# Search's end, the last maxima and eight modulation columns placed elsewhere on VectorE; TensorE multiplies constants in front of long waits

## What is computed

```python
for l in range(2):
    sh1, sc1, ga1, sh2, sc2, ga2 = split(silu(c) @ w_ada[l] + b_ada[l], 6)   # modulation, 48 columns of 128
    z = (rmsnorm(x, g1) * (1 + sc1) + sh1) @ w_in[l]
    a_out = u * (w_spatial @ standardize(v))        # chunked gating
    score = sum_h(wi[h] * relu(qi[h] @ ki.T))       # index scores, top 256 keys of each query are kept
    b_out = softmax(q @ k.T over the kept keys) @ v # prompt in blocks of 128, sampled rows over 2048 cached keys + 32
    c_out = silu(standardize(conv31(a * sigmoid(g))) * g_cn)
    x = x + ga1 * (concat(a_out, b_out, c_out) @ w_out[l])
    x = x + ga2 * ((silu(h2 @ w_gate) * (h2 @ w_up)) @ w_down)    # h2 = rmsnorm(x, g2) * (1 + sc2) + sh2
y = rmsnorm(x, g_final)
```

## Time and profile before

| | |
|---|---|
| median of 3 runs | 3053.58 us (3050.45 to 3053.7) |
| the profiled execution's own time | 3048.94 us |
| its span, first to last instruction | 3047.2 us |
| mean granted TensorE clock | 0.971 |
| PE busy | 2833.2 us (93%) |
| VectorE (DVE) busy | 1649.6 us (54%) |
| ScalarE (ACT) busy | 986.9 us (32%) |
| GpSimd (POOL) busy | 643.2 us (21%) |
| DMA queue of SP | 219.36 MB, 21.4% of 16 engines |

### The profile page before, as it was taken

How to read it: one execution, slowest core, us unless ns; L and a number is a source line. 1 busy time by engine, 2 the same in 40 slices (tenths; PEclk the granted TensorE clock), 3 DMA queues, 4 the chain that set the end, 5 groups by cost and what they waited for, 6 DMA issues and landing times.

```text
span 3047.2 us, 42621 instructions
## 1 busy us (share of the span) xinstructions
PE 2833.2 (93%) x15994; PEld 2448.6 (80%) x15994; DVE 1649.6 (54%) x2788; ACT 986.9 (32%) x1260; POOL 643.2 (21%) x278
## 2 busy tenths in 40 slices
PE   4998879889999999999979988898999999999996
PEld 2778733369999999999977875333999999999996
DVE  7768777683452444534544777763444335353355
ACT  4246646422221111111233564562332111111112
POOL 1411500001122222121242033000112222212221
PEclk9999989989999999999989999998999999999998
DMA  5412100251221222212241311002112222222222
GB/s 215 136 64 84 36 21 0 63 182 48 83 79 59 83 76 76 100 59 83 70 139 45 122 43 36 0 1 63 35 56 85 79 75 78 74 84 71 81 82 85
DMA packets 71352, 224.93 MB, mean 74 GB/s; under 512 B 17233, under 2 KB 17489, under 8 KB 70097
## 3 DMA queue, kind: packets, MB, share of 16 engines
q1 hardware_dynamic: 70192, 219.36, 21.4%
q10 hardware_dynamic: 1056, 4.19, 0.3%
HBM read 211.44 MB, written 11.54 MB: 73 GB/s over the span
## 4 chain that ended last, share of the span: by engine, by line
issue 45%; PE 35%; DVE 7%; ACT 6%; POOL 4%; DVEq 2%; DMA 1%; ACTq 0%; POOLq 0%; SPq 0%
PE ps L952 33%; ACT notsel L751 4%; POOL w_lo L591 4%; PE ps L998 1%; DVE hf L1344 1%; DMA w_ada<-in_w_ada 1%; PE ps L1059 1%; DVE ada_later L1363 1%; DVE ada_junk L1363 0%; DVE junk L1363 0%; DVE w_ada L1363 0%; DVE s_keep L1482 0%; DVEq L1472 0%; DVE s_cand L1470 0%; DVEq L1373 0%
## 5 line engine op out<-in xcount | busy, mean ns | idle before, releaser
L591 POOL TENSOR_TENSOR w_lo<-w_raw,w_hi 128x1024 fp32r<-128x1024 f32 x202 | 498.3, 2467 | 2282.3 <-ACT w_hi L702 2282.3
L952 PE MATMUL ps<-u_hi,w_hi 128*128 128x352 f32 (+1 forms) x2112 | 457.4, 325 | 2.1 <-ACT rstd L903 2.1
L952 PE MATMUL ps<-u_hi,w_lo 128*128 128x352 f32 (+1 forms) x2112 | 458.4, 325 | 0.0
L952 PE MATMUL ps<-u_lo,w_hi 128*128 128x352 f32 (+1 forms) x2112 | 455.6, 324 | 0.0
L702 ACT CAST w_hi<-w_raw 128x1024 fp32r<-128x1024 f32 x202 | 211.0, 1045 | 534.1 <-PE ps L952 314.6
L952 PEld LDWEIGHTS ps<-u_hi,w_hi 128*128 128x128 f32 x2112 | 362.1, 189 | 3.7 <-ACT rstd L903 2.7
L952 PEld LDWEIGHTS ps<-u_hi,w_lo 128*128 128x128 f32 x2112 | 361.0, 189 | 0.0
L952 PEld LDWEIGHTS ps<-u_lo,w_hi 128*128 128x128 f32 x2112 | 361.0, 189 | 0.0
L751 ACT ACTIVATE notsel<-score,s_cand 128x384 bf16<-128x384 f32 (+3 forms) x248 | 297.5, 1200 | 134.4 <-DVE s_cand L1470 134.3
L1778 DVE SCALAR_TENSOR_TENSOR x<-ps,mod,x 128x704 f32 (+2 forms) x240 | 125.4, 578 | 362.0 <-PE ps L952 355.6
L1363 DVE SCALAR_TENSOR_TENSOR junk<-w_ada,cond_row 128x1024 f32<-128x1024 f32 x104 | 219.9, 2114 | 26.8 <-issue 24.1
(11 more groups left out here) (261 smaller groups left out, 4120.3 us busy)
## 6 DMA issues: line engine op xcount, KB each, us to landing
w_ada<-in_w_ada SPq DMA_DIRECT2D x96, 512.0 KB, 4.9
w_raw<-in_w_up SPq DMA_DIRECT2D x88, 512.0 KB, 3.5
w_raw<-in_w_in SPq DMA_DIRECT2D x34, 512.0 KB, 3.6
ada_later<-in_w_ada SPq DMA_DIRECT2D x32, 512.0 KB, 3.5
cw<-in_convw SPq DMA_DIRECT2D x32, 512.0 KB, 5.2
w_raw<-in_w_down SPq DMA_DIRECT2D x32, 384.0 KB, 3.1
w_raw<-in_w_down SPq DMA_DIRECT2D x32, 320.0 KB, 2.9
w_raw<-in_w_out SPq DMA_DIRECT2D x16, 512.0 KB, 3.5
```

What stands on the lines that cost most here:

```text
L591: nc.gpsimd.tensor_tensor(w_lo[slot][:], w_raw[:], w_hi[slot][:].bitcast(F32), ALU.subtract)\
L952: last = nc.tensor.matmul(ps[:, bank + t, 0:w], wt[slot][:, kk, :], mv[:, kk, t * TW:t * TW + w], start=(at == 0 and p == 0), stop=(at == ...
```

## The change

- A helper `keep_warm(n, bank)` issues n products of 128x128 by 128x512 of bf16 constants into a bank of PSUM whose contents are not used. TensorE issues them: 16 in front of strip 0 of layer 0 (behind a new wait for the modulation), 26 in front of and 26 behind the sum of squares at the start of layer 1, 26 in front of the last one, and in each layer 14 in front of the waits of the index strip, 14 in front of the first mean (behind a new wait for the convolution's last group but one), and 5 in front of the third sampled chunk and 5 in front of the first transposed sampled chunk.
- `finish_search(0, PSRCH)` moves from between the two `gate_rows` to behind `diagonals(0)`. TensorE's wait for v_ready moves behind the first logits.
- In the sampled selection `diagonals(7)` moves to behind the scan, ahead of the selection's last three instructions. The filling of vcache with ones moves from VectorE to GpSimd.
- Layer 0's last eight modulation columns (the gate of the feed-forward part) leave the sampled stage: ten columns stand in front of the output of block 7 instead of thirteen, and six behind the first m_lo instead of eleven. The eight are made in the output projection, one behind each strip's u_lo, from a buffer of their own, and SP loads one behind each of the next weight strips (the first behind a wait for the last sampled product, the others behind a wait for the column before). Their bias is added behind the last, ahead of the signal that the sum of squares waits for.

```diff
@@ -104,6 +104,9 @@
+WARM_FIRST, WARM_SUM, WARM_NORM, WARM_INDEX, WARM_MEAN = 16, 26, 26, 14, 14
+WARM_SAMPLED, WARM_SAMPLED0 = 5, 5
 LN_EXP = "natural_log_exp_and_others"
@@ -122,6 +125,8 @@
+ADA_LATER = 48 - KD - ADA_FIRST
 ZB = 4352
@@ -261,6 +266,7 @@
         smax_s = small("smax_s", [P, 2, N_SL + 1], F32)
+        ada_gate = [place(f"ada_gate{s}", at[0] + s * 4 * D, [P, D], F32) for s in range(2)]
         probs = [small(f"probs{s}", [P, 2, 512], F32) for s in range(2)]
@@ -310,6 +316,8 @@
         later_used = signal("later_used", 0)
+        gate_loaded = signal("gate_loaded", 0)
+        gate_used = signal("gate_used", 0)
         ada_loaded = [signal(f"ada_loaded{s}", 24 * DMA) for s in range(2)]
@@ -417,6 +425,11 @@
+        def keep_warm(n, bank):
+            for _ in range(n):
+                nc.tensor.matmul(ps[:, bank, :], notsel_diag[:], neg_ident[:], start=True, stop=True)
@@ -543,20 +556,32 @@
                 if l == 0:
-                    load_later(ADA_STRIPS + 3, 48 - ADA_FIRST)
-                    sp.wait_ge(later_used.sem, 48 - ADA_FIRST)
+                    load_later(ADA_STRIPS + 3, ADA_LATER)
+                    sp.wait_ge(later_used.sem, ADA_LATER)
                     for d in range(4):
+                def load_gate(n):
+                    if l == 0:
+                        if n == 0:
+                            sp.wait_ge(pv_used.sem, pv_used.at(l, N_S + N_SS))
+                        else:
+                            sp.wait_ge(gate_used.sem, n)
+                        settle(sp)
+                        sp.dma_start(ada_gate[0][:], a["w_ada"][DEPTH - 1, 48 - KD + n]).then_inc(gate_loaded.sem, 16)
+                    load_gate(j - 2)
                     load_strip(FIRST_FF + e, a["w_up"][l, 0, e])
+                    load_gate(KD - 2 + e)
                 for g, nf in enumerate(GROUPS):
@@ -647,6 +672,8 @@
+                pool.wait_ge(sel_ready.sem, sel_ready.at(l, NSRCH))
+                nc.gpsimd.memset(vcache[:, :, :, HD:P], 1.0).then_inc(v_ones.sem, 1)
                 split_lo(FIRST_OUT + 1, 1)
@@ -986,7 +1013,12 @@
                 if l:
+                    keep_warm(WARM_SUM, 7)
                     rms(l, 0)
+                    keep_warm(WARM_NORM, 3)
+                else:
+                    pe.wait_ge(mod_ready.sem, mod_ready.at(l, 1))
+                    keep_warm(WARM_FIRST, 3)
@@ -1042,6 +1074,8 @@
                         pe.wait_ge(z_act.sem, z_act.at(l, COPIED.index(S_AV1) + 1))
+                        pe.wait_ge(conv_taken.sem, conv_taken.at(l, CONV_LOADS // 2 - 1))
+                        keep_warm(WARM_MEAN, 6)
                         pe.wait_ge(conv_taken.sem, conv_taken.at(l, CONV_LOADS // 2))
@@ -1076,6 +1110,7 @@
                     if j == S_QI1 + 2:
+                        keep_warm(WARM_INDEX, strip_bank(j))
                         pe.wait_ge(idx_rot.sem, idx_rot.at(l, 3))
@@ -1134,7 +1169,6 @@
                 nc.tensor.transpose(ps[0:DEC, 5, 0:P], vT[:, SEQ:TOK], ident).then_inc(v_turned.sem, 1)
-                pe.wait_ge(v_ready.sem, v_ready.at(l, 1))
                 pe.wait_ge(sp_taken.sem, sp_taken.at(l, 2))
@@ -1201,7 +1235,9 @@
                 late = None
-                for kind, n in ORDER:
+                for at, (kind, n) in enumerate(ORDER):
+                    if at == 1:
+                        pe.wait_ge(v_ready.sem, v_ready.at(l, 1))
                     if kind == "L":
@@ -1218,6 +1254,8 @@
                 for c, (c0, w) in enumerate(SAMPLE_CHUNKS):
+                    if c == 2:
+                        keep_warm(WARM_SAMPLED if l else WARM_SAMPLED0, 7)
                     if c >= 2:
@@ -1235,6 +1273,7 @@
                     if t == 0:
+                        keep_warm(WARM_SAMPLED, 7)
                         pe.wait_ge(nm_ready.sem, nm_ready.at(l, QB + 1))
@@ -1379,12 +1419,16 @@
-            def modulation(l, which, s0, s1):
+            def added(s0, s1):
+            def modulation(l, which, s0, s1):
+                added(s0, s1)
                 dve.drain()
@@ -1514,7 +1558,7 @@
-                def select(n, ranks):
+                def select(n, ranks, between=None):
@@ -1526,6 +1570,8 @@
                     nc.vector.tensor_tensor_scan(rk, ns, ns, 0.0, ALU.add, ALU.max)
+                    if between is not None:
+                        between()
                     dve.drain()
@@ -1660,7 +1706,6 @@
                 nc.vector.tensor_copy(q_samp[:].rearrange("p (b t) -> p b t", b=4), q[:, :, SEQ:TOK])
-                finish_search(0, PSRCH)
                 gate_rows(1)
@@ -1712,6 +1757,7 @@
                 diagonals(0)
+                finish_search(0, PSRCH)
                 for i in range(QB - 1):
@@ -1730,16 +1776,15 @@
                         finish_search(PSRCH, NSRCH)
-                        select(PSRCH, rank_samp).then_inc(sel_ready.sem, 1)
-                        dve.drain()
-                        nc.vector.memset(vcache[:, :, :, HD:P], 1.0).then_inc(v_ones.sem, 1)
-                    diagonals(i + 1)
+                        select(PSRCH, rank_samp, lambda: diagonals(QB - 1)).then_inc(sel_ready.sem, 1)
+                    else:
+                        diagonals(i + 1)
                     if i == 1:
                         start_search(PSRCH, NSRCH)
-                half = ADA_STRIPS + 13
+                half = ADA_STRIPS + 10
                 output(QB - 2, 2, P, (QB - 2) * P, (QB - 1) * P)
@@ -1762,11 +1807,11 @@
                 if l == 0:
-                    modulate_later(half, 48 - ADA_FIRST)
+                    modulate_later(half, ADA_LATER)
                 mixed_lo(M_LOW[1:2])
                 if l == 0:
-                    modulation(l, 1, 2, 6)
+                    modulation(l, 1, 2, 5)
                 mixed_lo(M_LOW[2:])
@@ -1800,6 +1845,13 @@
                         last.then_inc(u_ready.sem, 1)
+                        if l == 0:
+                            dve.wait_ge(gate_loaded.sem, (d * 2 + (e + 1)) * 16)
+                            modulate(ada_gate[0][:], d * 2 + (48 - KD + e), ada_gate[1]).then_inc(gate_used.sem, 1)
+                            dve.drain()
+                if l == 0:
+                    added(5, 6)
+                    dve.drain()
                 dve.sem_inc(sumsq_ready.sem, 1)
```

## The result

The changed kernel takes 3015.8 us (median of 4 executions, 3011.8 to 3017.1), the kernel before 3052.7 (median of 4, 3050.5 to 3053.7): ratio 0.988, 95% interval 0.987 to 0.989, 36.9 us less.

The account below looks back on a forecast made before the run. TensorE, busy 93% of the span, was taken as the bound, with time winnable at its waits for VectorE and the slow clock behind them; terms sum to -35.0 from 3048.94, 3013.9 profiled, 3018.6 as median, range 3004 to 3038.

Parts of the forecast that it names:

- Last maxima inside the selection: Eighth block, both layers: the next unit starts at the usual 3.78 us step; -8.9 in layer 0, -8.1 in layer 1.
- Eight columns out of the sampled stage: Layer 0's sampled stage: third sampled product starts near 619, full clock, m_lo wait gone; -16.8 us beyond the -8.9.
- Search's end behind the first maxima, both: Gating and first attention blocks: the wait is moved, not removed; +2.0 us a layer, +4.0 together, bounds -3 and +10.
- Sum of squares, layer 1: Start of layer 1: a wait of 8.78 us hides the constants, products run at the full clock level; -1.6 us.
- Final sum: Sum of squares at the end: a wait of 6.98 us hides the constants, products at full clock level; -1.9 us.
- Index strip, layer 1: Layer 1's index strip: no wait hides the fourteen constants and TensorE is full; +3.2 us, bounds 0 and +3.2.
- Sampled stage, layer 1: Layer 1's sampled stage: two times five constants keep the clock up; -4.9 us.
- Rival 1: Sampled stages and two sums: the constants do not keep the clock; 3034.4 us, chance 0.20.
- Rival 2: Index constants hide behind the search, moved search end costs nothing or gives; 3011.4 us, with means' gain 3006; chance 0.18.
- Rival 3: Loads: a cache or gate column lands late and SP's queue holds the weights; 3024 to 3029 us, chance 0.06.
- rival 5: The change does not do what it says, as when the fourth wait takes the third's place; near 3050, chance 0.02.
- rival 4: First attention blocks: the clock does not come back behind search's end; up to 38 us a layer, 3094, chance 0.04.

Follow-up runs that it names:

- run 7: The kernel before with only the eight modulation columns of layer 0 moved to the output projection: 3038.1 us.
- run 2: The changed kernel without the two times five constant products in the sampled stages: 3023.3 us.
- run 1: The changed kernel without any of its constant products, all moved steps staying: 3023.8 us.
- run 4: The changed kernel with the end of the first search back between the two gating rows: 3010.4 us.
- run 3: The changed kernel without the fourteen constants in front of the index strip, in both layers: 3011.9 us.
- run 6: The kernel before with only the eighth block's maxima spread inside the sampled selection and vcache's ones filled by GpSimd: 3036.5 us.
- run 10: The changed kernel with the first search's end back between the gating rows and no index strip constants: 3014.2 us (3004.4 to 3018.2).
- run 8: The changed kernel without the 26 constants in front of the sums of squares of layer 1 and the end: 3016.7 us (3016.5 to 3017.4).

## Why the prediction was right

The range (3004 to 3038) held, and 3018.6 is 2.8 us above the result; between the two profiled executions 35.0 less was said and 37.1 found. The terms, in the prediction's order, read as starts of the same instruction in both profiles:

| step | said | found |
|---|---|---|
| Last maxima inside the selection, layer 0 | -8.9 | -8.9 |
| the same, layer 1 | -8.1 | -8.1 |
| Eight columns out of the sampled stage | -16.8 | -16.8 |
| Search's end behind the first maxima, both | +4.0 | +1.2 between profiles, +4.4 by undoing it |
| Sum of squares, layer 1 | -1.6 | -1.6, in six profiles of nine |
| Final sum | -1.9 | -1.9 |
| Index strip, layer 1 | +3.2 | +3.0 |
| Sampled stage, layer 1 | -4.9 | -5.2 |

What no term named adds up to +1.2 us: layer 0's front came 1.0 us late, layer 1's strips behind the attention 0.6, and its index strip to gating 0.4 early.

**Last maxima.** Where the time is won was right to 0.1 us. Alone it is by the medians not worth 17 but 15.6: in layer 0 the third sampled product's wait grew to 7.57. The prediction used this implicitly, since it took that product's start from the columns, but its term reads as if it stood by itself. It does so only beside the columns' move. Maxima and columns alone, 15.6 and 13.6, the constants' 9.0 and the search end's -4.4 add up to 33.8, some 3 us less than all together. Of these, 2.3 us could be the growth of that wait; but four differences of medians scatter by as much, so that the parts help each other isn't shown.

**Eight columns.** The 16.8 consist of 10.1 for the move (run 7) and 6.7 for the constants (150.0, 140.0 and 133.2 us of the same stretch in before, run 2 and the change; run 1's profile, with 138.6, gives 5.3 for the constants); said were 9.4 and 7.4. The first sampled key product started at 614.9 and the third at 619.9, against 613.5 and 619 said; 1.3 of these differences had come about before the stage (577.35 for 576.01). The strips end at 0 cost, with 0.8 us to spare where 0.6 was said. VectorE's last column took 1.22 us, and POOL's last split ended at 741.7, before it, so the case that the rule of the Trainium skill (SBUF — State Buffer, Terms) describes didn't come up, and no run here shows what it would have cost. One thing was wrong: the wait for m_lo is not gone, 1.23 us of its 4.27 stay, and strip 17 takes 13.2 us instead of 12.5. The sampled part in front of it ended as much earlier than said (641.8 without the 1.3, for 642.5), so that the sum of 16.8 is exact partly by luck.

**Search's end.** The size stays open: +1.2 by two profiles, +2.3 in layer 1 alone by ten, +4.4 by the medians of run 4, all within the bounds. A difference of two single profiles is no measure for 2 us in a stretch where the clock falls at short waits. The mechanism held in part: the wait moved. But the prediction had TensorE standing some 8 us behind block 0 and slow only after that; it stood 4.77, for the clock had fallen already behind the 1.62 us in front of the first logits, which then took until 394.5 instead of 390. The wait got shorter by what the products got longer, and the selection began at 401.6, 1.3 us later than before, of which 1.0 had come about before the gating.

**Constants.** Rival 1 is out by runs 1 and 2. Its price, 15.8 us, was too high by the medians: without any constant the kernel is 9.0 us slower with the index strip's 3.0 gained, so 12.0. By the two profiled executions it was right, 12.1 in the sampled stages and 3.6 in the sums; which of the two holds in general isn't shown. The two times five in a layer, some 2.4 us of products, save 5 to 8 in the profiles of runs 1 and 2. Rival 2 is out by runs 3 and 4. Rival 3 left no trace, with no wait for w_lo or x in the projection, and rival 5 is out by the time. Of rival 4 there is a small trace: the clock from 400 to 450 us is 0.91, for 0.96 before, and 1.00 in run 4's profile.

## What to carry to other kernels

Look for short waits with narrow products behind them, not only for long ones: waits of 1.7 and 1.5 us cost 6.7 us in layer 0's sampled stage, most of it behind them, and ten throw-away products in front of them won that back. That it is the narrowness of the products isn't shown, since no run changed it; but the wait of 1.59 us in the attention, with products of values behind it, left the clock up in the change's profile (1.00 from 588 to 612 us). Throw-away work belongs where TensorE waits in any case and close to the wait's end; where it doesn't wait it costs its full time (3.0 us in layer 1's index strip), and with 3.16 us left idle behind it it helped in six profiles of nine, with 1.35 us left in all nine. Price moved work together with the wait that comes next: what came 5.7 us earlier to the sampled stage in run 6 waited 2.3 us longer there.

## What was not expected of the hardware

- One program, two clocks: behind the same wait of 3.16 us the same six products took 2.12 and 3.73 us in two executions. No instruction differs.
- The low level outlasts nearly full work by narrow products (most of them with 64 or 32 rows): in run 2 TensorE was busy 28.5 of 30.0 us at a mean of 0.72. The Trainium skill (TensorE: Matmul & The Clock Gate, A second HAM failure mode: psum-queue depth-cycling) tells of a kernel whose clock goes up and down by micro-idles between groups of matmuls; here it stayed down for some 16 us instead.
- Executions of one kernel on one chip lay 14 us apart (run 10), those of others 1 us (run 8).
